# Reordering the second mixer's panels, moving high parts to ScalarE, and filling head rows with zeros

## The reference

```python
# rmsnorm at each boundary: y = x * rsqrt(mean(x*x) + eps) * g
x = x + rmsnorm(mixed, post_mix_norm); h = rmsnorm(x, pre_mlp_norm)   # first block
x = x + rmsnorm(f, post_mlp_norm);     h = rmsnorm(x, norm_mix)       # into the second
# parallel_mixer
u, v_m, o_pre, i_pre, f_pre, c_q, c_kv, k_r = split(h @ w_in)
u_c = silu(causal_dwconv(u));  q_m, k_m = per-head products of u_c    # 4 heads, 64 wide
logf = log_sigmoid(f_pre);  b = cumsum(logf);  m = running max(i_pre - b)
w[t, s] = exp(gates of t and s) * (q_m[t] . k_m[s]) / 8,  s <= t
h_m = (w @ v_m) / max(|sum_s w|, exp(-m_t))
y_m = sigmoid(o_pre) * rmsnorm(h_m)
q_a = rmsnorm(c_q) @ w_uq;  kv = rmsnorm(c_kv) @ w_ukv;  y_a = causal attention
x = x + concat(y_m, y_a) @ w_out
# cross attention
h = rmsnorm(x, norm_x);  q = h @ wq_x;  k, v = split(rmsnorm(mem) @ wkv_x)
x = x + attention(q, k, v) @ wo_x
```

## Time and profile before

| | |
|---|---|
| median of 3 runs | 2048.9 us (2048.74 to 2050.75) |
| the profiled execution | 2052.12 us, span 2050.4 us |
| PE busy | 1935.8 us, 94% of the span |
| POOL busy | 1502.0 us, 73% |
| DVE, ACT busy | 861.7 us (42%), 693.3 us (34%) |
| mean granted clock | 0.965 |

### The profile page before, as it was taken

The page is one execution under the profiler, slowest core; times in us unless marked ns, Lnnn a source line. Parts: engine busy times, 40 slices in busy tenths (PEclk is TensorE's granted clock), DMA queues, the critical chain, the costliest instruction groups (busy, mean ns, idle before and its releaser), DMA issues.

```text
span 2050.4 us, 26465 instructions
## 1 busy us (share of the span) xinstructions
PE 1935.8 (94%) x9771; PEld 1626.2 (79%) x9771; DVE 861.7 (42%) x1700; ACT 693.3 (34%) x1326; POOL 1502.0 (73%) x1345
## 2 busy tenths in 40 slices
PE   6999999999999999989999998989888989999998
PEld 4888888887878887768888886886667878888887
DVE  3576666652014543455403414543453164402411
ACT  3466666653015562132102202366531141100100
POOL 6799888787863446878888988640349628988984
PEclk9999999999999999989999998998799899999999
DMA  6322222222332222412333232211012303333332
GB/s 214 92 62 63 62 62 62 62 62 82 97 96 79 61 76 67 139 47 91 94 102 101 84 103 72 78 52 42 25 46 96 102 3 100 101 88 99 102 97 68
DMA packets 213068, 165.68 MB, mean 81 GB/s; under 512 B 14447, under 2 KB 209330, under 8 KB 212579
## 3 DMA queue, kind: packets, MB, share of 16 engines
q1 hardware_dynamic: 207286, 147.35, 24.4%
q10 hardware_dynamic: 5676, 16.95, 2.5%
HBM read 161.11 MB, written 7.37 MB: 82 GB/s over the span
## 4 chain that ended last, share of the span: by engine, by line
PE 79%; POOL 13%; DVE 4%; ACT 3%; issue 2%; DMA 0%; DVEq 0%; SPq 0%; ACTq 0%; POOLq 0%
PE bank L390 56%; PE bank L437 7%; POOL w_lo L2676 5%; POOL w_hi L2671 4%; PE bank L1361 3%; PE bank L1337 2%; PE bank L409 2%; PE bank L1347 1%; POOL x_features L674 1%; POOL arena L1054 1%; PE bank L1036 1%; PE bank L483 1%; PE bank L2208 1%; PE bank L1014 1%; DVE arena L579 1%
## 5 line engine op out<-in xcount | busy, mean ns | idle before, releaser
L2676 POOL TENSOR_TENSOR w_lo<-w_raw,w_hi 128x512 fp32r<-128x512 f32 (+2 forms) x592 | 737.1, 1278 | 81.2 <-ACT w_hi L1199 68.9
L2671 POOL TENSOR_TENSOR w_hi<-w_raw,one 128x512 fp32r<-128x512 f32 (+1 forms) x492 | 507.0, 1062 | 359.2 <-PE bank L390 333.4
L390 PE MATMUL bank<-h_hi,w_hi 128*128 128x512 f32 (+1 forms) x1056 | 420.7, 398 | 14.7 <-POOL w_lo L2676 9.3
L390 PE MATMUL bank<-h_hi,w_lo 128*128 128x512 f32 (+1 forms) x1056 | 409.9, 388 | 0.0
L390 PE MATMUL bank<-h_lo,w_hi 128*128 128x512 f32 (+1 forms) x1056 | 409.0, 387 | 0.0
L390 PE MATMUL bank<-a_hi,w_hi 128*128 128x512 f32 x848 | 333.2, 393 | 11.2 <-POOL w_lo L2676 6.8
L390 PE MATMUL bank<-a_lo,w_hi 128*128 128x512 f32 x848 | 331.8, 391 | 0.0
L390 PE MATMUL bank<-a_hi,w_lo 128*128 128x512 f32 x848 | 331.7, 391 | 0.0
L390 PEld LDWEIGHTS bank<-h_hi,w_hi 128*128 128x128 f32 x1056 | 202.3, 192 | 54.6 <-POOL w_lo L2676 10.6
L390 PEld LDWEIGHTS bank<-h_hi,w_lo 128*128 128x128 f32 x1056 | 201.9, 191 | 40.6
L390 PEld LDWEIGHTS bank<-h_lo,w_hi 128*128 128x128 f32 x1056 | 202.6, 192 | 35.4
(11 more groups left out here) (419 smaller groups left out, 2825.6 us busy)
## 6 DMA issues: line engine op xcount, KB each, us to landing
w_raw<-in_w_ff SPq DMA_DIRECT2D x32, 1024.0 KB, 5.4
w_raw<-in_w_in SPq DMA_DIRECT2D x31, 1024.0 KB, 5.3
w_raw<-in_w_mlp_in SPq DMA_DIRECT2D x16, 1024.0 KB, 5.3
w_raw<-in_w_mlp_out SPq DMA_DIRECT2D x16, 1024.0 KB, 5.6
w_raw<-in_w_in SPq DMA_DIRECT2D x26, 512.0 KB, 4.4
w_raw<-in_w_ssd_out SPq DMA_DIRECT2D x8, 1024.0 KB, 5.5
bias_rows<-bias_row ACTq DMA_DIRECT2D x1, 4096.0 KB, 15.8
w_raw<-in_w_attn_out SPq DMA_DIRECT2D x4, 1024.0 KB, 5.0
```

The lines of the kernel that those rows point to most:

```text
L390: mm = pe.matmul(bank[:, 0:ntok], a, b[:, koff + k, 0:ntok], start=(k == 0 and n == 0), stop=(k == L.kb - 1 and n == 2))
L2671: pool.tensor_tensor(w_hi[:, slot, part], raw[:, slot, part], one[:].broadcast_to([P, n]), ALU.mult).then_inc(split_hi, 1)
L2676: ins = pool.tensor_tensor(w_lo[:, slot, part], raw[:, slot, part], w_hi[:, slot, part].bitcast(F32), ALU.subtract)
```

## The change

1. The gate panel `L_if` moves from the third place to behind the values, and the two panels of values become `L_va` (in front of `L_low`) and `L_vb` (behind it). ScalarE makes the high parts of `L_va`, `L_low` and `L_vb`.
2. The gates' softplus (`gates_dve`, `gates_act`) moves behind the second block of `L_uq`; the row scans (`gate_rows_dve`) move behind the key sums. ScalarE copies the scans' inputs out of PSUM first, and the exponential of the fourth row is taken after its transpose (on 16 columns and 128 partitions, not on a row of 512).
3. `square_dve` leaves out the last block of each norm, and `root_sum_pe` runs eight matmuls, four of them on that block's squares.
4. ScalarE makes the high part of the second panel behind each of the two norms (`post_act`), and of `L_out2` 2 and 3, `L_kvx` 0 to 3 and `L_qx` 0 and 1 (`cross_act`).
5. POOL writes a copy of each head's queries with the other head's 64 rows zero (`heads_query_pool`), and the scores contract over 128 partitions. The decay rows stand in a tile of 128 rows, zero but for four.

```diff
-        L_if = Linear(1, DB, P, [0], lambda i: w_in2[:, :, IF0:IF0 + P])
+        L_va = Linear(1, DB, 256, [0, 128], column_panels(w_in2, 512, 1))
...
-        L_v = Linear(2, DB, 256, [0, 128], column_panels(w_in2, 512, 2))
+        L_vb = Linear(1, DB, 256, [0, 128], column_panels(w_in2, 768, 1))
+        L_if = Linear(1, DB, P, [0], lambda i: w_in2[:, :, IF0:IF0 + P])
...
         def square_dve(dve, b):
             nx_n["acc"] += 1
+            if b == DB - 1:
+                return
...
         def root_sum_pe(pe):
             nx_n["sum"] += 1
-            pe.wait_ge(nx_acc, DB * nx_n["sum"])
+            pe.wait_ge(nx_acc, (DB - 1) * nx_n["sum"])
+            pe.wait_ge(nx_sq, DB * nx_n["sum"])
             for t in range(T):
-                mm = pe.matmul(banks[4][:, t:t + 1], NACC[:, t * P:(t + 1) * P], one[:], start=True, stop=True)
+                tok = slice(t * P, (t + 1) * P)
+                pe.matmul(banks[4][:, t:t + 1], NACC[:, tok], one[:], start=True, stop=False)
+                mm = pe.matmul(banks[4][:, t:t + 1], NSQ[(DB - 1) % 2][:, tok], one[:], start=False, stop=True)
...
         def post_act(act, n, gain):
+            split_high_act(act, (L_mlp[0][0][0], L_u)[n], 1)
             root_act(act)
...
-        HIGH_BY_ACT = list(range(L_ssd[1][1].p0, L_gate_ssd.p0)) + [L_low.p0, L_v.p0, L_v.p0 + 1] + [L.p0 for L in L_gate_m]
+        HIGH_BY_ACT = list(range(L_ssd[1][1].p0, L_gate_ssd.p0)) + [L_mlp[0][0][0].p0 + 1, L_u.p0 + 1] + [L.p0 for L in (L_va, L_low, L_vb, *L_gate_m)] + [L_out2.p0 + 2, L_out2.p0 + 3] + list(range(L_kvx.p0, L_qx.p0 + 2))
...
         def mlstm_qk_pe(pe, h):
-            p0 = 64 * (h % 2)
+            pe.wait_ge(ml["padded"], h + 1)
...
-                pe.matmul(QK_RING[u % 3][:, 0:S - bs * P], KM[p0:p0 + 64, h // 2, bs * P:(bs + 1) * P], QM[p0:p0 + 64, h // 2, bs * P:S],
+                pe.matmul(QK_RING[u % 3][:, 0:S - bs * P], KM[:, h // 2, bs * P:(bs + 1) * P], Q_PADDED[:, h, bs * P:S],
...
-            pe.matmul(banks[7][:], ident[0:4, h:h + 1].broadcast_to([4, P]), ROW[1], start=True, stop=True).then_inc(ml["bc"], 1)
+            pe.matmul(banks[7][:], ident[:, h:h + 1].broadcast_to([P, P]), DECAY_ROWS, start=True, stop=True).then_inc(ml["bc"], 1)
...
+        def heads_query_pool(pool):
+            pool.wait_ge(acc_free, L_low.b0 + T // 2 + M_HEADS)
+            pool.wait_ge(lt["turn"], 6)
+            pool.wait_ge(lt["red"], 4 * T)
+            for h in range(M_HEADS):
+                rows = (m_lt[:, 64:65], m_gt[:, 63:64])[h % 2].bitcast(F32)
+                pool.tensor_tensor(Q_PADDED[:, h, :], QM[:, h // 2, :], rows.broadcast_to([P, S]), ALU.mult).then_inc(ml["padded"], 1)
...
         def cross_act(act):
-            unscaled_act(act, "norm_x", counted(acc_free, L_out2.b0), a_upper_x, slow=True)
+            for b in range(DB):
...
+                if b % 2:
+                    split_high_act(act, *((L_out2, 2), (L_out2, 3), (L_kvx, 0), (L_kvx, 1))[b // 2])
+            root_act(act)
             for b in range(DB):
                 kvx_act(act, b)
+                if b % 2:
+                    split_high_act(act, *((L_kvx, 2), (L_kvx, 3), (L_qx, 0), (L_qx, 1))[b // 2])
```

More of the change, by code:

```diff
@@ L2120, in mlstm_pe @@
             pe_panel_tokens(pe, L_cq, 0, 0, h_x)
[L2121 to L2127 removed]
+            pe_panel_tokens(pe, L_va, 0, 0, h_x)
+            pe_panel_tokens(pe, L_low, 0, 0, h_x, width=LOW_W)
             pe.wait_ge(sp_lo, 4)
@@ L2136, in mlstm_pe @@
                 mm.then_inc(acc_ready, 1)
[L2138 to L2146 removed]
+            pe_panel_tokens(pe, L_vb, 0, 0, h_x)
+            pe_panel(pe, L_if, 0, 0, h_x)
             pe.wait_ge(lt["low"], 1)
```

134 lines of the change are left out of this document (72 added, 62 removed).

## The result

The changed kernel takes 2017.97 us (median of 4 runs, 2016.77 to 2019.67) and the kernel before 2049.82 us on the same chip (4 runs, 2048.74 to 2051.17): a ratio of 0.984, 95% interval 0.9825 to 0.9855. The profiled execution of the changed kernel took 2016.77 us with a span of 2015.1, against 2052.12 and 2050.4.

What follows compares the result with a forecast made beforehand. It took TensorE, busy 1935.8 of 2050.4 us, as the bound, with 114.6 us idle and slow-clock slices to win. Terms -2.8 + 1.0 - 8.9 - 13.0 - 9.7 = -33.4 gave 2015 us; range 2008 to 2030, a little over 8 in 10.

Steps and rivals of the forecast that it cites:

- Norms, -2.8: Behind first mixer and first MLP: ScalarE's high parts let POOL's adds begin 1.2 and 1.6 us earlier, together -2.8 us.
- Sums, +1.0: Eight sum matmuls: gain and cost cancel at four places where TensorE waits; in front of the last MLP they cost 1.0.
- The mixer's order, -8.9: Second mixer to first score: 14.2 us of waits and half clock go, new waits cost 5.3, net -8.9.
- a: Second mixer: `L_uq` waits for ScalarE's high parts and VectorE's last low part behind the low ranks' transposes, 1.7 us.
- b: Second mixer: the softplus behind two blocks of `L_uq` keeps its banks from being freed, a new wait of 1.2 us.
- c: Second mixer: row copies and the sigmoid's table load delay the gate panel's evacuation, `L_gate_m[1]` and `L_ukv`, 1.5 us.
- Heads, -11.5: Four heads: matmuls over 128 partitions raise the clock, halving later scores and products, -11.5 us.
- Attention's start, -1.5: The attention behind the heads no longer begins at the low clock: -1.5 us, by judgment between 0 and -2.
- Output to query panels, -9.7: ScalarE's high parts cut waits from 13.8 to 7.4, half clock from 6 to 1.7; extra sum matmuls +1.0; net -9.7 us.
- the clock in the heads rose: Rival: the heads' clock stays low because busyness counts or zero rows count as empty; 13.0 us go, 2028.5; chance 0.16.
- the handoffs ate 3 us: Rival: the longer PE, ScalarE, POOL chain eats gains in mixer (-3) and cross attention (-4); 2027 us; chance 0.13.
- TensorE did not fall to the lower clock: Rival, slower: TensorE falls to 1.2 GHz between `L_if` and the first score and stays low; 2065 us; chance 0.03.

Runs made afterwards that it cites:

- norm_pool: The changed kernel with POOL, not ScalarE, making the high parts behind both norms again; 2017.08 us, 0.9839 of the kernel before.
- old_sums: The changed kernel with VectorE adding the eighth square again and four matmuls making the sum at all norms; 2021.86 us, 0.9844 of the kernel before.
- old_order: The kernel before with all parts of the change except the second mixer's new order; 2023.47 us, 0.986 of the kernel before.
- best: split_first with halved high parts at norms and cross attention, and VectorE's eighth add at the last two norms; 2007.16 us, 0.979 of the kernel before.
- cross_pool: The changed kernel with POOL making the eight high parts of L_out2 2 and 3, L_kvx and L_qx again; 2030.16 us, 0.9893 of the kernel before.
- split_first: The changed kernel with ScalarE's cross-attention high parts put before its copies, squares, root and evacuations in odd blocks; 2010.92 us, 0.9795 of the kernel before.
- no_fill: The changed kernel with scores over 64 partitions, decay row over 4, and no padded queries; 2025.31 us, 0.9869 of the kernel before.

## Why the prediction was right

The mechanisms were in the main the ones forecast, and the total (-33.4) is right: -33.9 over the stretches, -31.9 between the medians. Two terms failed (the sums and the attention's start), and two were off by their clock (the mixer's order and the panels). Its terms:

- **Norms, -2.8.** 1.33 and 1.70 us at POOL's adds; 2.5 us when taken out (norm_pool). Right.
- **Sums, +1.0.** A gain of about 2.1 by old_sums. "At these four places gain and cost cancel, within half a us each" is the step that failed: a wait for the last add of about 1 us drew a fall of the clock at one of its two places in each trace (0.98 yes, 1.04 no before; 1.07 yes, 0.69 no in old_sums), 1.7 us each, which I didn't count. Nor did "Extra sum matmuls +1.0" at the query panels come: TensorE waits right behind them anyway. In front of the last MLP they cost 0.55.
- **The mixer's order, -8.9.** 8.2 by itself. The stretch as a whole gave 12.0; the missing item is again clock behind waits: of the 3.8 between, 3.4 are the two falls that are gone or halved with the other edits. The new waits that I priced at 5.3 us are 0.4 + 0.9 (a, forecast 1.7), 1.3 (b, 1.2), 1.3 (c, 1.5; 0.8 of it waited before), 0.2, and 0.75 for the row scans: about 4 us more than stood before. Of the scans, "so they cost nothing" is wrong by those 0.75 us: it looked at ScalarE's queue, and not at POOL's copies beside them.
- **Heads, -11.5.** -12.2; a head every 7.2 us against 7.4, products in 2.40 us. The padding alone is worth 11.0 in the heads, 10.3 with what its copies cost the scans. The rule that it hung on, matmuls over few partitions let the clock fall, holds as a whole; that the scores alone do it would have been too simple.
- **Attention's start, -1.5.** Nothing: stretch 5 is 152.75 us with the heads filled and 152.76 without. The clock is low there for one stretch in both, and what TensorE waits for at the attention's start (2.67 us, ScalarE) is as long as before. This term was a judgment without a row, and it failed. Where the attention did gain 1.1 us, by one fall less (old_sums, old_order, best), nothing in it was edited.
- **Output to query panels, -9.7.** 6.3 by cross_pool, 6.7 between the traces. The waits are right (7.9 against 7.4). The step that failed is "half clock remains behind the first wait alone: 1.7", 4.3 us gained, where 0.9 were (6.5 us lost before, 5.6 after): the wait of 1.56 us for `L_kvx` 1 lets it fall a second time, and 5.6 us are lost. split_first shows it: the wait taken away, the clock stays at 1.00 there.

So the misses of the mixer and the sums on one side cancelled those of the attention and the panels on the other. That the total is better than its parts is luck. The parts also don't add. Taken out one at a time they are worth 2.5 + 2.1 + 8.2 + 11.0 + 6.3 = 30.1 us at their own places, and 30.0 over all stretches (2.4 - 0.8 + 7.1 + 10.1 + 11.2); together 33.9. The 3.8 between are as much as the mixer's stretch gave beyond its order, but falls of the clock that move by 1 to 5 us between traces are in each of these sums. The rivals: the clock in the heads rose (no_fill against the changed kernel); the handoffs ate 3 us between the output and the query panels, as clock behind the wait of 1.56 us, and none in the mixer; and TensorE did not fall to the lower clock in the stretch of small matmuls in front of the scores.

## What to carry to other kernels

Price a wait of TensorE with the stretch at the lower clock that may stand behind it: here waits of 1.0 and 1.6 us cost 1.7 and 2.9 more. It is a risk and not a rule, since waits of 1.04, 1.28 and 1.30 us had no fall behind them. Where its matmuls go over 64 or 4 partitions and the granted clock is 0.50 at full occupation, fill them with zeros to 128: it gave 11 us in 42. Place the copies where no one near the critical path works beside them; here they lengthened VectorE's scans and cost 0.75 us. When a helper engine takes over a step in a chain, put the step in front of that engine's other work, and judge edits of a few us from one untouched mark to the next, since the part that nobody changed moves by more than they do. Then look whether the difference lies where the edit is.
